# Spreading the transposes of bk over three insertions in a chunked RWKV-7 inverse, with its copy one step later

## What is computed

```python
def step(S, inp):
    r_t, w_t, k_t, v_t, kk_t, b_t = inp
    sa = jnp.einsum('bhvk,bhk->bhv', S, -kk_t)
    S = S * w_t[:, :, None, :] + sa[..., None] * b_t[:, :, None, :] + v_t[..., None] * k_t[:, :, None, :]
    y = jnp.einsum('bhvk,bhk->bhv', S, r_t)
    return S, y
```

## Time and profile before

| what | value |
|---|---|
| median of 3 runs | 1326.67 us (1326.63 to 1329.27) |
| the profiled execution | 1325.83 us, its span 1324.0 us |
| granted TensorE clock, mean | 0.993 of full speed |
| TensorE products busy | 1287.6 us, 97% |
| VectorE busy | 723.1 us, 55% |
| ScalarE busy | 699.1 us, 53% |
| GpSimd busy | 306.6 us, 23% |

### The profile page before, as it was taken

The page is one execution under the profiler, slowest core; times in us unless marked ns, Lnnn a source line. Parts: engine busy times, 40 slices in busy tenths (PEclk is TensorE's granted clock), DMA queues, the critical chain, the costliest instruction groups (busy, mean ns, idle before and its releaser), DMA issues.

```text
span 1324.0 us, 24437 instructions
## 1 busy us (share of the span) xinstructions
PE 1287.6 (97%) x9453; PEld 1113.9 (84%) x9453; DVE 723.1 (55%) x1671; ACT 699.1 (53%) x1683; POOL 306.6 (23%) x234
## 2 busy tenths in 40 slices
PE   7999999999999999999999999999999999999996
PEld 7989798897979889798797878888898888778885
DVE  5356867768676776868664543334443445540013
ACT  6446767666666766667655543445344444432321
POOL 3430000010000101000002333433434334334443
PEclk8999999999999999999999999999999999999998
DMA  6322111211112121121212222222222222236333
GB/s 225 91 68 63 56 52 57 60 56 51 57 56 61 49 63 53 57 58 49 65 52 78 73 64 80 73 68 68 85 71 70 79 80 71 73 96 231 96 96 141
DMA packets 151523, 102.35 MB, mean 77 GB/s; under 512 B 6414, under 2 KB 140912, under 8 KB 149872
## 3 DMA queue, kind: packets, MB, share of 16 engines
q1 hardware_dynamic: 151408, 100.79, 25.6%
HBM read 96.57 MB, written 4.19 MB: 76 GB/s over the span
## 4 chain that ended last, share of the span: by engine, by line
PE 83%; DVE 7%; ACT 5%; issue 3%; DMA 1%; SPq 0%; POOL 0%; DVEq 0%; ACTq 0%
PE tile L598 49%; PE tile L884 2%; PE tile L886 2%; PE tile L885 2%; PE ma L854 2%; PE ma L720 1%; PE mb L869 1%; PE mb L804 1%; PE ma L729 1%; PE ma L884 1%; PE ma L886 1%; PE ma L885 1%; PE mb L884 1%; PE mb L886 1%; PE mb L885 1%
## 5 line engine op out<-in xcount | busy, mean ns | idle before, releaser
L598 PE MATMUL tile<-hn_hi,w_hi 128*128 128x264 f32 (+2 forms) x1664 | 435.8, 324 | 0.0
L598 PE MATMUL tile<-hn_hi,w_lo 128*128 128x264 f32 (+2 forms) x1664 | 429.0, 320 | 0.0
L598 PE MATMUL tile<-hn_lo,w_hi 128*128 128x264 f32 (+2 forms) x1664 | 426.5, 319 | 0.0
L1313 POOL TENSOR_TENSOR w_lo<-w_raw,w_hi 128x512 fp32r<-128x512 f32 x196 | 258.5, 1322 | 421.2 <-ACT w_hi L983 421.0
L598 PEld LDWEIGHTS tile<-hn_hi,w_hi 128*128 128x128 f32 x1664 | 270.4, 189 | 29.1 <-issue 11.3
L598 PEld LDWEIGHTS tile<-hn_hi,w_lo 128*128 128x128 f32 x1664 | 270.0, 189 | 13.7 <-issue 1.7
L983 ACT CAST w_hi<-w_raw 128x512 fp32r<-128x512 f32 x324 | 199.4, 616 | 155.3 <-PE tile L598 60.0
L598 PEld LDWEIGHTS tile<-hn_lo,w_hi 128*128 128x128 f32 x1664 | 269.8, 189 | 9.9 <-issue 0.2
L1328 POOL TENSOR_TENSOR arena<-arena,power 128x10 f32<-128x10 f32 (+3 forms) x28 | 44.2, 1579 | 577.1 <-DVE arena L1506 443.6
L1159 ACT ACTIVATE arena<-ma 64x192 f16<-64x192 f32 x240 | 77.9, 325 | 56.1 <-PE ma L720 54.6
L1168 ACT ACTIVATE arena<-ma 128x384 f16<-128x384 f32 x120 | 58.8, 490 | 68.5 <-PE ma L761 67.5
(11 more groups left out here) (257 smaller groups left out, 2169.5 us busy)
## 6 DMA issues: line engine op xcount, KB each, us to landing
w_raw<-w_in SPq DMA_DIRECT2D x260, 256.0 KB, 2.8
w_raw<-w_out SPq DMA_DIRECT2D x64, 256.0 KB, 3.0
big<-x SPq DMA_DIRECT2D x4, 1024.0 KB, 7.2
arena<-x SPq DMA_DIRECT2D x4, 1024.0 KB, 8.7
out<-big SPq DMA_DIRECT2D x3, 1024.0 KB, 3.9
arena<-post_norm_w SPq DMA_DIRECT2D x1, 1024.0 KB, 5.0
out<-big SPq DMA_DIRECT2D x2, 512.0 KB, 3.8
arena<-table_rope SPq DMA_DIRECT2D x2, 264.0 KB, 3.0
```

Of the source, the lines that this page charges most:

```text
L598: last = mm(o[:, at:at + n], w[:, slot, cols], t[:, kt, tok:tok + n], start=(kt == 0 and w is w_hi and t is hn_hi), stop=(kt == KT - 1 and ...
L1313: T(w_lo[:, slot, :], w_raw[:, slot, :], w_hi[:, slot, :].bitcast(F32), ALU.subtract).then_inc(s("lo_done"), 1)
```

## The change

On TensorE the transposes of bk of a group no longer stand together behind line 736. One chunk is turned behind line 736, the second behind the three products of line 750 of level 1 (behind the raising of `zz_done`), the third behind the three of line 761 of level 1 (behind `x_done`). The last group has no third one. Each transpose now raises `bk_turned` by itself, so that it counts chunks (8 per tile) and no longer groups (3 per tile).

On ScalarE the wait for `bk_turned` and the copy to bk_tok move from behind line 1147 to behind line 1168 of level 1. TensorE's wait for `bk_taken` stays in level 2, ahead of the first line 720.

On VectorE the place of the wait ahead of the new bk stays; only its value is counted in chunks: i * SC in place of i * NG. So it is met when the last chunk of the present tile has been turned.

```diff
 # inv_pe
+                def turn_bk(c):
+
+                    if cs[c] < SC:
+                        nc.tensor.transpose(bank(1, c), bk[:, cs[c], :], ident).then_inc(s("bk_turned"), 1)
...
                 last.then_inc(s("t0_done"), 1)
-                for c in range(GC):
-                    if cs[c] < SC:
-                        last = nc.tensor.transpose(bank(1, c), bk[:, cs[c], :], ident)
-                last.then_inc(s("bk_turned"), 1)
+                turn_bk(0)
                 for l in range(1, LEVELS):
                     yield level_at(g, l, 0)
...
                         last = mm(half(ma, c), bl(lv, (l - 1) * GC + c), single(x16, c), start=True, stop=True)
                     last.then_inc(s("zz_done"), 1)
+                    if l == 1:
+                        turn_bk(1)
                     if l == 2:
                         pe.wait_ge(s("bk_taken"), n)
...
                         last = mm(half(ma, c), bl(xt16, c), half(z16, c), start=True, stop=True)
                     last.then_inc(s("x_done"), 1)
+                    if l == 1:
+                        turn_bk(2)
 # inv_act
                 A(x_twice, x_made, ACT.Copy).then_inc(s("t0_taken"), 1)
-                act.wait_ge(s("bk_turned"), n)
-                if i > 1:
-                    act.wait_ge(s("s_done"), states_so_far(i - 1, min((g + 1) * GC, SC) - 1))
-                w = min(GC, SC - g * GC) * P
-                A(bk_tok[g][:, 0:w], ma[:, 512:512 + w], ACT.Copy).then_inc(s("bk_taken"), 1)
...
                     act.wait_ge(s("x_done"), n * 5 + (l - 5))
                     A(x_twice, x_made, ACT.Copy).then_inc(s("x_taken"), 1)
+                    if l == 1:
+                        act.wait_ge(s("bk_turned"), (i - 1) * SC + min((g + 1) * GC, SC))
+                        if i > 1:
+                            act.wait_ge(s("s_done"), states_so_far(i - 1, min((g + 1) * GC, SC) - 1))
+                        w = min(GC, SC - g * GC) * P
+                        A(bk_tok[g][:, 0:w], ma[:, 512:512 + w], ACT.Copy).then_inc(s("bk_taken"), 1)
 # stage_dve
                 if i:
-                    dve.wait_ge(s("bk_turned"), i * NG)
+                    dve.wait_ge(s("bk_turned"), i * SC)
```

## The result

| | before | changed |
|---|---|---|
| median, us | 1326.57 (7 runs, 1325.76 to 1329.27) | 1331.30 (7 runs, 1330.50 to 1332.34) |
| the profiled execution's span, us | 1324.0 | 1330.3 |
| granted TensorE clock, mean | 0.993 | 0.993 |

The ratio is 1.0036, with a 95% interval of 1.0024 to 1.0048: slower by 4.7 us.

The account below looks back on a forecast made before the run. TensorE sets the pace for most of a tile, VectorE for about 12 us around the last group's first steps; VectorE's 0.80 us stalls less TensorE's savings give +4.1 us, so 1330.8 us, range 1326.5 to 1333.5.

Parts of the forecast that it names:

- A transpose's cost: On TensorE: one transpose behind half-precision products costs 0.05 us, each further one 0.11; a first group saves 0.12.
- rival 1: On TensorE: a float32 transpose costs 0.11 us wherever it stands, nothing is saved; +5.6 us, 1332.3; chance 0.12.
- The group norm's insertion: Second group, line 761 of level 1: the moved transpose makes four five, costing 0.11 us; the group saves 0.06.
- The copy: ScalarE's later copy of bk costs nothing, about 0.5 us to spare before line 720; 0.1 us allowed for tile 1.
- Rival 3: Line 720 waits for ScalarE's late copy, 0.1 us in each of 24 groups: +2.4 on top, 1333.2; chance 0.08.
- DVE's wait: Last group, ahead of the new bk (line 1561): DVE stands still 0.80 us until the second transpose is done.
- What queues behind it: On DVE, lines 1561, 1586, 1561, 1650 follow without a gap, so PE's line 761 comes 0.80 us later; nothing gives it back.
- Rival 2: Last group: DVE's wait costs nothing or DVE recovers before line 1650; PE savings alone, -2.0 us, 1324.7; chance 0.12.
- The sum: Tile 1 +0.66, tiles 2 to 7 +0.62 each, tile 8 -0.24: together +4.1 us, 0.3%.
- Period from tile to tile: At line 761, the distance from one tile to the next grows from 78.5 to about 79.1 us.

Follow-up runs that it names:

- e1: The change made in groups 0 and 1 only, last group as in the kernel before: 1325.62 us against 1326.59, ratio 0.9992.
- e2: The change made in the last group only, groups 0 and 1 as in the kernel before: 1334.05 us, ratio 1.0052.
- e4: The whole change, with VectorE's w_lo ahead of the wait for the transposes, no longer behind the new bk's first half: 1328.09 us, ratio 1.0013 against the kernel before.
- e5: The whole change, with the w_lo of place 46.6 made at place 42.2: 1327.36 us, ratio 1.0006 against the kernel before.
- e3: The kernel before with only ScalarE's copy of bk moved behind the copy of level 1, in all groups: 1327.28 us, ratio 1.0004.
- e8: Change in groups 0 and 1 only, w_lo at place 42.2, new bk's second half behind level 1's product copy: 1322.42 us, ratio 0.9964 against the kernel before.

## Why the prediction was right

The forecast was 1330.8 us, a range of 1326.5 to 1333.5 and 0.72 for slower; measured were 1331.3. The mechanism was the one named: e1 and e2 put the whole loss on the last group, and e4 and e5 show that it comes through DVE's queue. Its terms can be checked one by one.

- **A transpose's cost.** 0.05 was taken for a single one behind half-precision products, between 0.03 and 0.11; it is 0.06 in all three places. That makes a first group's saving 0.09 in place of 0.12 (the traces' 0.07 to 0.10), and rival 1, no saving, is out: e1 wins 0.91 over seven tiles where it would have won nothing. The spacing of the further transposes of a run was 0.11. The Trainium skill ("TensorE: Matmul & The Clock Gate", LDWEIGHTS) puts a weight load of 128 columns at 107 ns, and the 0.11 of the further ones agrees with it; the single transpose, with 0.06, takes less. The recorded weight load of line 726 is 0.14 us, so a part of it lies beside the neighbours; which part was not tried.

```profile
L726 PEld LDWEIGHTS ma<-c,arena x64: 138/141/143, 95.4 to 696.8; 128*128 128x128 f32 x64
```

- **The group norm's insertion.** A fifth transpose in it costs 0.12 (0.50 against 0.38), forecast 0.11; the second group saves 0.04 in place of 0.06.
- **The copy.** Forecast at nothing, with 0.1 for tile 1; e3 measured nothing, with 0.06 for tile 1, which did not fall to the group that the forecast named. Rival 3 is out.
- **DVE's wait.** Forecast 0.80 a tile, measured 0.93 (the new bk starts 0.90 later against the first step; DVE's instruction ahead of it ended 0.03 earlier). Nearly all of the difference is one term of the sum: for the time from the recorded end of the transpose to DVE's start I took 0.04, from a row of ScalarE, and it is 0.14 (383.95 to 384.09). DVE's wait for `bk_turned` is an instruction of its own, line 1566, which only DVE's sequencer handles. It is recorded from 384.00 on, 0.04 behind the transpose, and lasts 0.05; line 1568 starts 0.05 behind it. Its rows, all seven, and that of tile 4:

```profile
L1566 DVEq EVENT_SEMAPHORE  x7: 49/49/50, 146.2 to 621.8; - x7
```

```profile
L1566 DVEq EVENT_SEMAPHORE  x1: 50/50/50, 384.0 to 384.0; - x1
```

Before, the same instruction (line 1559) ran at 380.9, beside line 1554, and cost nothing. The rest is as forecast within 0.01: the 0.11 that PE comes earlier, the transpose's start 0.10 behind the first product and its record of 0.30.
- **What queues behind it.** The four instructions and their distances stayed, and PE's wait in front of line 765 grew by 0.95, forecast 0.80. Nothing gave it back, as said. Rival 2, in which DVE catches up, is out by the trace, and e4 and e5 show the chain by shortening it.
- **The sum.** Forecast +4.1; by the traces +5.28 up to the first group of tile 8, where the forecast has +4.4 (0.66 and six times 0.62); the medians say +4.7. The part that was too small is seven times the 0.1 behind the transpose and some 0.04 a tile of the transposes' cost.

Period from tile to tile: 79.1 was forecast, and DVE's start behind the wait recurs every 79.26 us (146.32 in tile 1 to 621.88 in tile 7). What the median has below the trace's sum lies in the scatter of the runs.

## What to carry to other kernels

When a step is moved later, follow every wait that counts it, also those on engines that the change doesn't mean to touch: here a saving of a tenth of a microsecond on the busiest engine was paid with 0.9 on another, because a second reader of the same signal, VectorE beside ScalarE, stood in its queue ahead of work that the busiest engine needs. A wait that is an instruction of its own adds its own time once the engine really stands at it, here 0.1 us. Ask for each stretch of a period which engine sets the pace in it: TensorE was 97% busy, and yet the largest gain, 4.2 us by the trace, came from taking 0.7 us of VectorE's work per tile out of the one stretch in which TensorE waits for it. Parts of a change should be tried apart, for e1 keeps the small gain that the whole change hides.

## What the runs showed that I had not expected

The trace of the changed kernel has 1.4 us of its 6.3 in a place that the change doesn't touch: between 742 and 750 us of the kernel before, the distance of the two traces grows from 4.98 to 6.39. Behind tile 8, PE stands idle for 2.04 us in front of line 867 (a wait in the attention part; 2.00 before in front of the same line, 861 there), and from about 1.3 us after that (line 867 starts at 747.23) its granted clock is at 0.50 for 3.4 us, the lower of its two levels, 1.2 GHz. The windows of the changed kernel, columns: stretch; length; busy time and instructions of PE, PEld, DVE, ACT and POOL; granted clock; DMA share; GB/s:

```profile
749.00:750.00 1.00, 1.00 (x7) 1.00 (x6) 0.15 (x1) 0.80 (x2) 0.00 (x0) 0.50 0.51 151
750.00:751.00 1.00, 1.00 (x6) 0.99 (x5) 0.00 (x0) 0.98 (x2) 0.00 (x0) 0.50 0.00 0
```

The kernel before, with the same idle time, has 1.00 there:

```profile
743.00:746.00 3.00, 3.00 (x24) 2.76 (x23) 1.06 (x2) 1.90 (x5) 0.00 (x0) 1.00 0.40 117
```

e1 and e3 have the fall too, at the same place and for the same 1.4 us, e2 and e4 to e8 don't, so it goes neither with the change nor with the time. It may be a part of the scatter of 1 to 3 us among the runs of one kernel; what decides it was not tried. It is a reason to compare two such traces tile by tile and not by their spans: e2's is only 0.2 us longer than the changed kernel's, and its median is 2.8 above.

The 0.14 us between a float32 transpose and DVE's start belong neither to DVE nor to the transpose. Behind the four float32 transposes of line 883, which raise one signal, DVE's line 1771 starts 0.04 after their recorded end, eight times in eight. There the separate instruction (line 1770) waits for another signal and is done at 790.3, over a microsecond before, and line 1771 itself waits for the transposes:

```profile
791.07 0.66 PE L883 MATMUL ma<-c,arena 128*128 128x128 f32 x4
```

```profile
791.76 0.75 DVE L1771 SCALAR_TENSOR_TENSOR big<-gate,gate_sub,ma 128x512 f32<-128x512 f32 x1 [0.75 <-PE ma L883]
```
